# Conditioning products in other places, narrower blocks in two HGRN levels, and the first q and f products side by side

## The reference

```python
# second block: the conditioning vector's products (two layers, 1024 x 6144 each)
cond = jax.nn.silu(c)
for i in range(DEPTH):
    mod = cond @ ada_w[i] + ada_b[i]
    sh1, sc1, g1, sh2, sc2, g2 = jnp.split(mod, 6)
    h = rms_norm_2(x, mix_norm_g[i]) * (1.0 + sc1) + sh1
    ...
    x = x + g1 * y
    h = rms_norm_2(x, mlp_norm_g[i]) * (1.0 + sc2) + sh2
    x = x + g2 * (jnp.square(jax.nn.relu(h @ mlp_w1[i])) @ mlp_w2[i])

# first block, layer 0: a unit lower triangular solve for each head and chunk
sol = triangular_solve(low + I, rhs)

# first block, layer 1 (HGRN2), for each head; decay is the product of the gates between s and t
q_raw, f_raw, i_in, z = jnp.split(x @ w_in, 4)
attn[t, s] = sum_d q[t, d] * k[s, d] * decay[t, s, d]      # for s <= t
o = attn @ v + ...
```

## Time and profile before

| | us |
|---|---|
| median of 3 runs | 1400.9 |
| lowest and highest of them | 1396.63, 1404.89 |
| the profiled execution, its own time | 1390.31 |
| its span from first to last instruction | 1388.4 |
| mean granted clock of TensorE in it | 0.985 |

### The profile page before, as it was taken

One profiled execution on the slowest core, in us unless ns is written; L12 is line 12 of the kernel. 1 busy time (PEld: TensorE's weight loads), 2 busy tenths in 40 slices (PEclk: granted clock), 3 DMA queues, 4 the chain that ended last, 5 costly groups with the idle time before them and its releaser, 6 DMA issues.

```text
span 1388.4 us, 27551 instructions
## 1 busy us (share of the span) xinstructions
PE 1319.2 (95%) x11904; PEld 1217.3 (88%) x11904; DVE 958.3 (69%) x1503; ACT 737.9 (53%) x993; POOL 23.4 (2%) x55
## 2 busy tenths in 40 slices
PE   6998997899989999999899997999999999999998
PEld 5997887799989999999798875988888998988887
DVE  4878867645466788777654696788777776676543
ACT  6666243246544555555245424687534786587531
POOL 0000000000000000000000000000000000000000
PEclk9999899999999999999899999999999999999999
DMA  6555563544265555555232324468875333455551
GB/s 256 183 177 217 196 232 123 199 168 156 97 255 186 197 197 192 206 208 186 92 122 92 123 93 155 164 233 299 302 273 192 143 126 127 143 182 182 196 198 62
DMA packets 34648, 247.35 MB, mean 178 GB/s; under 512 B 3872, under 2 KB 3872, under 8 KB 4960
## 3 DMA queue, kind: packets, MB, share of 16 engines
q1 hardware_dynamic: 29968, 213.35, 43.2%
q0 software_dynamic: 4560, 32.25, 6.6%
HBM read 244.53 MB, written 1.05 MB: 177 GB/s over the span
## 4 chain that ended last, share of the span: by engine, by line
PE 82%; DVE 8%; ACT 6%; issue 3%; DMA 1%; DVEq 0%; ACTq 0%
PE PS L475 14%; PE PS L417 10%; PE PS L418 9%; PE PS L419 9%; PE PS L476 7%; PE PS L490 6%; PE PS L899 3%; ACT WH L550 3%; DVE WL L563 2%; PE PS L433 2%; PE PS L435 2%; PE PS L434 2%; PE PS L963 2%; PE PS L456 1%; PE PS L457 1%
## 5 line engine op out<-in xcount | busy, mean ns | idle before, releaser
L563 DVE TENSOR_TENSOR WL<-RAW,WH 128x2048 fp32r<-128x2048 f32 x166 | 380.1, 2290 | 121.4 <-ACT WH L550 118.1
L550 ACT ACTIVATE WH<-RAW 128x2048 fp32r<-128x2048 f32 x166 | 317.0, 1909 | 177.8 <-PE PS L476 70.0
L417 PE MATMUL PS<-XW,WH 128*128 128x256 f32 x1024 | 301.6, 295 | 16.6 <-DVE WL L563 12.3
L418 PE MATMUL PS<-XW,WH 128*128 128x256 f32 x1024 | 293.3, 286 | 1.0 <-issue 1.0
L419 PE MATMUL PS<-XW,WL 128*128 128x256 f32 x1024 | 293.2, 286 | 0.0
L417 PEld LDWEIGHTS PS<-XW,WH 128*128 128x128 f32 x1024 | 200.4, 196 | 19.0 <-DVE WL L563 12.3
L419 PEld LDWEIGHTS PS<-XW,WL 128*128 128x128 f32 x1024 | 199.7, 195 | 1.1 <-issue 1.1
L418 PEld LDWEIGHTS PS<-XW,WH 128*128 128x128 f32 x1024 | 200.3, 196 | 0.2
L475 PE MATMUL PS<-XW,WH 128*128 128x512 f32 x392 | 141.0, 398 | 0.2
L297 DVE SCALAR_TENSOR_TENSOR BIG<-BIG,C 128x256 f32<-128x256 f32 (+2 forms) x228 | 101.3, 504 | 29.9 <-ACT BIG L1309 13.5
L476 PE MATMUL PS<-XW,WL 128*128 128x256 f32 x392 | 110.0, 280 | 0.0
(11 more groups left out here) (388 smaller groups left out, 2584.8 us busy)
## 6 DMA issues: line engine op xcount, KB each, us to landing
RAW<-wst SPq DMA_DIRECT2D x200, 1024.0 KB, 4.9
BIG<-wad POOLq DMA_DIRECT2D x30, 1024.0 KB, 5.1
X<-xT SPq DMA_DIRECT2D x1, 1024.0 KB, 4.8
outT<-X SPq DMA_DIRECT2D x4, 256.0 KB, 4.1
K<-cst SPq DMA_DIRECT2D x1, 608.0 KB
CB<-crow SPq DMA_DIRECT2D x1, 512.0 KB
BIG<-pT POOLq DMA_DIRECT2D x2, 256.0 KB, 3.9
C<-cols SPq DMA_DIRECT2D x1, 370.0 KB
```

The costliest lines, as they stand in the source:

```text
L417: pe.matmul(o, h, hl[0][:, k0 + k, :], start=(k == 0), stop=False)
L418: pe.matmul(o, h, hl[1][:, k0 + k, :], start=False, stop=False)
L550: ac.activation(WH[p % NS][:, :], RAW[u % NR][:, :], ACT.Copy).then_inc(S.hi.tick(p), 1)
L563: ve.tensor_tensor(WL[p % NS][:, :], RAW[u % NR][:, :], WH[p % NS][:, :].bitcast(f32), ALU.subtract).then_inc(S.lo.tick(p), 1)
```

## The change

1. The 48 conditioning pieces get other places. The table ADA_BESIDE names the indices of FILL behind whose split a piece stands: 3 to 9, 11, 13, 15, 17, 19, 21 and 23, where before it was 2 to 19. The stream thus has 14 pieces and not 18. The HGRN layer (16) and the first MLP (14) keep their places, with pieces of lower number. The last four pieces stand in the last MLP, after the products w1 with n of 1, 3, 5 and 7; GpSimd fetches them after the norm before that MLP. Of layer 1, `ve_mods` now adds the bias to 40 columns, and a new instruction behind the last piece adds it to the 8 columns of g2.
2. At level 5 the matmul takes just the blocks that are copied: for each of four m and of two offsets a, 32 columns of k by 32 of q, into partitions a to a+32. At level 6 it takes 64 columns of k and 64 of q.
3. The first products q and f of the HGRN layer are made by a new function `stagger`: k of 0 to 5 of q, k of 0 to 5 of f, then k of 6 and 7 of q, then of f. On VectorE the split of f's weight is moved ahead of `gate(3)`.

```diff
 LEVELS = 7
-STREAM_ADA = 18
+ADA_BESIDE = (3, 4, 5, 6, 7, 8, 9, 11, 13, 15, 17, 19, 21, 23)
 QK = [(w, n) for n in range(4) for w in range(2)]
-SIDE_ADA = 34
+STREAM_ADA, SIDE_ADA, LAST_ADA = len(ADA_BESIDE), 30, 44
 AT = {}
...
         add(key, spec)
-        if 2 <= i < 2 + STREAM_ADA:
-            ada_after[where[key]] = (i - 2, len(units))
-            units.append(("ada_w", 0, 0, 256 * (i - 2)))
+        if i in ADA_BESIDE:
+            n = ADA_BESIDE.index(i)
+            ada_after[where[key]] = (n, len(units))
+            units.append(("ada_w", 0, 0, 256 * n))
     turn[1] = 3
...
                             t.then_inc(S.mm.tick(key, n), 1)
+        def stagger(pe, keys, hl, cut, ready):
+            for part in (range(cut), range(cut, 8)):
+                for key in keys:
+                    b = bank_of[key]
+                    if part[0] == 0:
+                        pe.wait_ge(*S.lo(where[key]))
+                        vacate(pe, b, key)
+                    wh, wl = (w[where[key] % NS][:, :].rearrange("p (k n) -> p k n", k=8) for w in (WH, WL))
+                    for k in part:
+                        if key == keys[0]:
+                            ready(k)
+                        for n in range(2):
+                            o = PS[b][:, n * T:(n + 1) * T]
+                            h, l = wh[:, k, n * 128:(n + 1) * 128], wl[:, k, n * 128:(n + 1) * 128]
+                            pe.matmul(o, h, hl[0][:, k, :], start=(k + n == 0), stop=False)
+                            pe.matmul(o, h, hl[1][:, k, :], start=False, stop=False)
+                            t = pe.matmul(o, l, hl[0][:, k, :], start=False, stop=(k == 7 and n == 1))
+                            if k == 7:
+                                t.then_inc(S.mm.tick(key, n), 1)
...
             gp.wait_ge(*S.norm.ac("rstd", "cln"))
-            for n in range(SIDE_ADA, 48):
+            for n in range(SIDE_ADA, LAST_ADA):
+                side(n)
+            gp.wait_ge(*S.norm.ac("rstd", "r3"))
+            for n in range(LAST_ADA, 48):
                 side(n)
...
             vacate(pe, b, "lv", hp, lv)
-            if 0 <= lv < 7:
+            if lv == 5:
+                for m in range(4):
+                    for a in (0, 64):
+                        ks, qs = k[:, m // 2, 128 * (m % 2) + a:128 * (m % 2) + a + 32], q[:, m // 2, 128 * (m % 2) + a + 32:128 * (m % 2) + a + 64]
+                        t = pe.matmul(PS[b][a:a + 32, 64 * m + a // 2:64 * m + a // 2 + 32], ks, qs, start=True, stop=True)
+            elif lv == 6:
+                for m in range(4):
+                    c = 128 * (m % 2)
+                    t = pe.matmul(PS[b][0:64, 64 * m:64 * m + 64], k[:, m // 2, c:c + 64], q[:, m // 2, c + 64:c + 128], start=True, stop=True)
+            elif 0 <= lv < 7:
                 qs = by_blocks(q, 1 << lv)
...
             if hp == 0:
-                product(pe, ("q", 0), XHL, 0, lambda k: pe.wait_ge(*S.al("x1", k // 2)))
-            for w in ("q", "f", "v", "z")[0 if hp else 1:]:
+                stagger(pe, [("q", 0), ("f", 0)], XHL, 6, lambda k: pe.wait_ge(*S.al("x1", k // 2)))
+            for w in ("q", "f", "v", "z")[0 if hp else 2:]:
                 for n in range(2):
...
                 gate_opened(3)
+                then(ve, ("gate", 0, 2))
                 gate(3)
-                then(ve, ("gate", 0, 2))
                 low(3)
...
         def ve_mods(ve, i):
-            m = MOD[:, 48 * i:48 * i + 48]
-            ve.wait_ge(*S.ada(24 * i + 23))
-            ve.tensor_tensor(m, m, col("ada_b", 48 * i, 48), ALU.add).then_inc(S.mod.ve.tick("add", i), 1)
+            c = 8 * (LAST_ADA - 24) // 4 if i else 48
+            m = MOD[:, 48 * i:48 * i + c]
+            ve.wait_ge(*S.ada(LAST_ADA - 1 if i else 23))
+            ve.tensor_tensor(m, m, col("ada_b", 48 * i, c), ALU.add).then_inc(S.mod.ve.tick("add", i), 1)
             ve.wait_ge(*own("ve"))
...
         def ve_mlp(ve, i, Lnext):
-            a = SIDE_ADA
+            a = LAST_ADA if i else SIDE_ADA
             for n in range(16):
...
                 ve.tensor_tensor(HW[n][:, 1, :, :], r, HW[n][:, 0, :, :].bitcast(f32), ALU.subtract).then_inc(S.al.tick("h", i, n), 1)
-                if i == 0 and n % 2:
+                if n % 2 and a < 48:
                     side_ada(ve, a)
                     a += 1
+                    if a == 48:
+                        ve.wait_ge(*S.ada(47))
+                        ve.tensor_tensor(mod(1, 5), mod(1, 5), col("ada_b", 88, 8), ALU.add).then_inc(S.mod.ve.tick("last"), 1)
             for n in range(4):
...
                     then(ve, key)
-                    if i == 0 and kb % 2 and a < 48:
+                    if i == 0 and kb % 2 and a < LAST_ADA:
                         side_ada(ve, a)
```

## The result

| | kernel before | changed kernel |
|---|---|---|
| median of the runs | 1400.0 us (4 runs, 1396.6 to 1404.9) | 1380.2 us (4 runs, 1379.4 to 1381.4) |
| profiled execution | 1390.3 us, span 1388.4 | 1380.4 us, span 1378.1 |
| idle time of PE in the span | 69.2 us | 58.8 us |

The ratio is 0.986, with a 95% interval of 0.983 to 0.989: faster by 19.8 us in this comparison, where 13.9 were forecast, and 1380.2 us lies at the lower edge of the range. Three of the four runs of the kernel before are the three behind the 1400.9 us of the prediction and come from another time than those of the changed kernel. Two later comparisons, each with all its runs on one chip, gave 14.9 and 15.8 us. Why three comparisons of the same two programs differ by 5 us is the second half of the lesson.

A forecast was written before the change was run, and what follows sets the result against it. PE was taken as the bound, busy 1319.2 of 1388.4 us. Terms of 4.95, 6.45 and 2.5 us summed to 13.9, taking the median from 1400.9 to 1387.0 us, range 1380 to 1396.5.

The forecast's parts named there:

- Part 1: Conditioning pieces moved in the solve and to the last MLP: gain 4.95 us, between 3 and 5.5.
- Index 2: Solve, piece at 100.4 us in a chain through DVE: removing it gains 2.3 us, 1.56 to 2.75.
- Index 14: Solve, piece at 234.85 us ahead of PE's 2.42 us wait: removing it gains 2.3 us.
- Index 10: Solve, piece ahead of a subtraction that PE waits 0.35 us for: removing it gains 0.35 us.
- Indices 12, 16 and 18: Solve, pieces with no PE wait behind them, since DVE then waits for PE: removing them gains nothing.
- Part 3: q beside f: the 4.35 us stall and 2.1 us of slow clock go, 6.45 us gained, at least 4.
- Part 2: Narrower levels 5 and 6, eight pairs of heads: gain 2.5 us, between a loss of 2.5 and a gain of 4.
- rival D: Level 5: changing array columns drains like a tile change, kernel 8.6 us slower at 1409.5 us; chance 0.04.
- A: Solve: ACT is next to be late and takes the gain up, 2.5 us instead of 4.95; chance 0.15.
- B: Level 5: records come at the pace of 64 columns, so Part 2 loses 2.5 us; chance 0.1.
- C: q and f: split too late or clock falls, gap not fully closed, 4 us instead of 6.45; chance 0.1.
- E: Whole kernel: slow clock in the solve goes too and levels gain 4 us, 17 us in all, 1384; chance 0.07.

The follow-up runs named there:

- levels: Kernel before with only the narrower levels 5 and 6: median 1391.56 us, ratio 0.997 to the kernel before.
- pieces: Kernel before with only the conditioning pieces dealt out anew: median 1393.91 us, ratio 0.998 to the kernel before.
- side_by_side: Kernel before with only q and f by stagger and f's weight split ahead of gate(3): median 1389.50 us, ratio 0.9945.
- piece14: Kernel before with one conditioning piece moved from the split of index 14 to that of index 23: one execution, 1398.9 us against 1397.3 before.
- last_pair: Changed kernel with one conditioning piece in the last pair of heads moved behind level 2's selection: median 1376.34 us, ratio 0.9847 to the kernel before.
- whole_again: The changed kernel run once more beside its three parts on one chip: median 1381.36 us, ratio 0.988 to the kernel before.
- both_moves: Changed kernel with the piece of index 3 moved behind index 12 and the last_pair move: median 1374.56 us, ratio 0.9832 to the kernel before.

## Why the time spreads, and where the missing part of the forecast was

The kernel before ran 28 times in the first comparison, between 1390.0 and 1404.2 us, with a granted clock between 0.970 and 0.984 as mean over the span. Over these runs time and clock go together: the correlation is -0.90, and 0.01 of clock are 8.4 us. In the 12 runs of `levels` it is -0.96 and 10.2 us, in those of `pieces` -0.92 and 11.4; in the 11 of `side_by_side` it is looser, -0.63 and 4.7. (Such a correlation does not show by itself which of the two sets the other.) What differs can be seen in the solve, where side_by_side and levels have the same instructions as before. From split 3 to split 41 it takes 358.7 us in before and 365.9 in side_by_side (windows, columns as in the earlier trace rows):

```profile
33.90:392.60 358.70, 330.85 (x4193) 316.48 (x4192) 246.76 (x396) 179.87 (x256) 2.80 (x5) 0.98 0.48 173
```

```profile
32.80:398.70 365.90, 341.69 (x4193) 327.18 (x4192) 246.92 (x396) 179.85 (x256) 2.81 (x5) 0.93 0.48 170
```

The counts are the same, VectorE's and ScalarE's busy times agree within 0.2 us, and only PE's work takes 10.8 us longer, at 0.93 instead of 0.98. So 7 us lie between two executions of one and the same stage, as much as the largest term of the forecast. The clock falls mostly during or soon after idle times of PE of 1 us or more, in the solve, in the last pair of heads, around 850 us and around 1170 us, but not at each of them and not at the same ones each time. One fall, at 193.5 us in the changed kernel, has no idle time of over 0.2 us in the 16 us ahead of it. What decides it in one execution I can't say from these runs.

## Where the prediction failed, and where it was right

*Part 1, 4.95 us.* Index 2: forecast 2.3, measured 2.29, and of the wait at 126 us 0.47 us went, so the gain was that of one piece, and not the 2.75 of both waits. Index 14: forecast 2.3, measured 1.8 at split 27 and 2.4 at split 28 in the changed kernel, and 1.7 and 2.1 alone (piece14). Index 10: forecast 0.35, and 0.2 us can be seen. Indices 12, 16 and 18, the two added in the solve and the four in the last MLP cost and gave nothing: where a piece stands behind index 23, split 36 comes some 1.8 us late, the late landing that was thought possible, and split 37 is in time again. VectorE's splits come up to 2.3 us later in the last MLP than the lead by then, which is made good again before its end, and PE has no new wait: the cover that was named holds. In sum 4.1 us are left at the end of the solve in `pieces`, where the clock has its share, and the changed kernel is ahead by 4.7 us at split 28.

*Part 3, 6.45 us.* Measured 6.68. The wait of 0.3 us for the split that was thought possible did not come. The clock's part in it holds in all traces here: it fell at this wait in each of the six that have it (4.3 to 4.8 us idle), and in none of the eight where q and f alternate.

*Part 2, 2.5 us.* This term was too small. Level 6 was to take 0.94 us and takes 0.93. Level 5 was to take 0.83 and takes 0.70. Two numbers in its sum were too large: the 15 intervals between loads are 0.015 us each (0.22 in all), where I had weighed 0.01 against 0.028 and taken 0.02, and the way out is 0.15 us and not the 0.20 taken over from the 64*64 row. The profile names its tile 128*32, as I had taken it; level 6 has 128*64, where I had only the 64*64 row, and that price held. Seven pairs of heads gave 0.42 us each, 2.9 instead of 1.9. In the last pair PE's steps from the product's last matmul to what follows level 7, in the kernel before and in last_pair, where the clock was full as well:

```profile
691.35 0.28 PE L419 MATMUL PS<-YW,WL 128*128 128x256 f32 x1
...
696.46 0.49 PE L871 MATMUL PS<-BIG 128*128 128x128 f32 x2 [0.47 <-ACT BIG L1474]
```

```profile
672.91 0.28 PE L420 MATMUL PS<-YW,WL 128*128 128x256 f32 x1
...
677.19 0.49 PE L897 MATMUL PS<-BIG 128*128 128x128 f32 x2 [0.47 <-ACT BIG L1509]
```

They take 5.11 us and 4.28, so 0.8 instead of 0.6. In all 3.8 us, just under the upper bound of 4. The way into the other tile costs 0.32 us (441.21 to 441.53), as the rows said. That agrees with the drain that the Trainium skill ("TensorEngine Tiling (Array Packing)", Key Properties) names for a change of the mode. Changing the column within it costs no drain: level 5 changes it with each matmul and the loads of a matmul follow those of the one before by 0.03 us, so rival D was out. The prediction's estimate from the 60 cycles of overhead for each matmul that the same page (Instruction Overhead) has made level 5 take 0.9 us, and the trace has 0.70. That does not decide against the page: the estimate charged its 25 ns to each of the 16 records, while a matmul is two of them. Charged once for each of the eight matmuls it gives 0.53 + 7 x 0.025 = 0.7 us, again an estimate, which level 5 can't tell from its own 0.70.

*The sum.* Read where the clock is the same, the terms measure about 4.1 to 4.7, 6.7 and 3.8 us, so some 15, against 13.9 forecast and 14.9 and 15.8 in the two comparisons with many runs.

*The step that failed* is the first one, the starting point: "the median of the runs is 10.6 us longer, and I take the difference over to it unchanged". The profiled execution of before was one of the fastest that this kernel gives (1390.3, with 1390.0 the lowest of 28), and the three runs of 1396.6 to 1404.9 us were from the slower half. The 10.6 us between them are no property of the kernel: against the median of many runs the profiled execution lies 5.9 us below in before, 3.9 below in pieces, 6.3 below in levels, 1.6 above in side_by_side and 1.2 above in whole_again. From 1396.2 us, the median of the 28, the forecast of 13.9 gives 1382.3, and the changed kernel measured 1381.4 beside them; from 1398.1, the median of the 11, it gives 1384.2 against 1382.3. So of the 6.8 us between the forecast 1387.0 and 1380.2, the starting point is 2.8 to 4.7, part 2 is 1.3, and the rest is not told apart. The range had next to nothing for such draws: the terms' bounds gave 1385 to 1396, and it adds 5 us below and 0.5 above. Of the 20 us of gain in the first comparison about 15 are the change. The other 5 are most likely what the two sets of four runs happened to draw (all four of before lie above the median of the 28), or their chip or time, which the runs don't tell apart. The rivals A, B and C were not at work; E named the right direction for a part of it, but slow clock in the solve did not go (the clock falls in the same stage in all traces of the changed kernel).

## What to carry to other kernels

Where an engine's work stands in a row ahead of a wait, take out one piece at a time and measure again: the first gave its whole 2.3 us, the next 1.5, since another engine was by then a step behind. Two edits can need each other: the order of the products was worth 4.8 us without the moved split and 6.7 with it, and the split alone nothing. And before a forecast is added to a measured time, ask how far single runs of that kernel lie apart, and with what: here runs of one program lay 14 us apart, mostly in step with the granted clock, so that three runs fix the starting point worse than the profile fixes the change.

## What the hardware showed that I had not expected

- Weight loads of 32 columns in a 128*32 tile follow each other every 0.015 us in level 5, 16 of them, for eight matmuls, in 0.38 us with the way back to the full array (441.53 to 441.91), though they change between two columns of tiles. A level of half that count in 128*64 tiles takes 0.61 us (444.97 to 445.58).
- Runs of one program on one core spread by 1%, and in most kernels here the time goes with the mean granted clock (0.970 to 0.984 in the 28 runs of before, 8.4 us for 0.01; 4.7 to 11.4 in the others).
- With one wait of PE shorter by 2.3 us the clock stayed at 1.00 for 50 us in one execution (last_pair) and not in another with the same edit (both_moves).
